# Two-layer encoder with mixture of experts on one Trainium2 core: VectorE forms the low parts of an expert's weights a whole unit at a time

## What is computed

```python
for l in range(DEPTH):
    xn = rms_norm(x, attn_norm[l])
    proj = xn @ w_in[l]
    ...
    x = x + mixed @ w_out[l]
    x = x + moe_ffn(rms_norm(x, ffn_norm[l]), w_router, router_bias, w_gate[l], w_up[l], w_down[l])

def moe_ffn(h, w_router, router_bias, wg, wu, wd):
    ...
    hg = jnp.einsum('nd,edf->nef', t, wg)
    hu = jnp.einsum('nd,edf->nef', t, wu)
    act = jax.nn.silu(hg) * hu * combine[:, :, None].astype(t.dtype)
    out = jnp.einsum('nef,efd->nd', act, wd)
```

## Time and profile before

| | us |
|---|---|
| median of 3 runs | 1950.42 (1948.66 to 1955.75) |
| the profiled execution | 1956.39 |
| its span, first to last instruction | 1954.2 |
| PE busy | 1848.6 |
| DVE busy | 1581.5 |
| ACT busy | 1438.5 |
| mean granted clock of TensorE | 0.974 |

### The profile page before, as it was taken

One profiled execution on the slowest core, in us unless ns is written; L12 is line 12 of the kernel. 1 busy time (PEld: TensorE's weight loads), 2 busy tenths in 40 slices (PEclk: granted clock), 3 DMA queues, 4 the chain that ended last, 5 costly groups with the idle time before them and its releaser, 6 DMA issues.

```text
span 1954.2 us, 30129 instructions
## 1 busy us (share of the span) xinstructions
PE 1848.6 (95%) x8762; PEld 1494.0 (76%) x8762; DVE 1581.5 (81%) x2248; ACT 1438.5 (74%) x2279; POOL 104.6 (5%) x86
## 2 busy tenths in 40 slices
PE   7999999997999999989999999999979999999998
PEld 6887888886677777778778878888867777777775
DVE  5566777657999999999974667775589999999998
ACT  5465666445899999899765646664468999999995
POOL 0000000001010111000000000000010110100000
PEclk9999999996999999999999999999979999999999
DMA  7654444565999999999856444345569999999997
GB/s 271 212 186 141 161 162 155 183 230 201 380 420 420 421 422 421 422 421 419 346 209 243 155 151 161 141 173 194 215 237 409 420 421 421 421 420 418 421 420 270
DMA packets 86699, 582.07 MB, mean 298 GB/s; under 512 B 13612, under 2 KB 13868, under 8 KB 18896
## 3 DMA queue, kind: packets, MB, share of 16 engines
q1 hardware_dynamic: 75600, 542.01, 70.4%
q0 software_dynamic: 11008, 38.95, 5.3%
HBM read 575.91 MB, written 29.36 MB: 310 GB/s over the span
## 4 chain that ended last, share of the span: by engine, by line
PE 58%; DMA 14%; DVE 10%; issue 10%; ACT 7%; ACTq 0%; DVEq 0%; SPq 0%; POOL 0%; POOLq 0%
PE bank L877 12%; PE bank L879 11%; PE bank L878 11%; DMA proj<-in_expert_units 8%; DMA raw<-in_expert_units 5%; PE bank L1032 4%; PE bank L1034 4%; DVE wl L1232 3%; ACT wh L590 3%; PE bank L1051 2%; PE bank L1053 2%; PE bank L1052 2%; DVE xl L1232 2%; PE bank L1023 2%; ACT rows L807 1%
## 5 line engine op out<-in xcount | busy, mean ns | idle before, releaser
L1224 DVE TENSOR_TENSOR wl<-raw,wh 128x1024 fp32r<-128x1024 f32 x256 | 310.1, 1222 | 229.9 <-ACT wh L581 229.6
L581 ACT ACTIVATE wh<-raw 128x1024 fp32r<-128x1024 f32 x256 | 269.0, 1056 | 268.5 <-PE bank L879 266.3
L877 PE MATMUL bank<-wh,xh 128*128 128x512 f32 x1024 | 417.1, 407 | 2.5 <-DVE wl L1224 2.4
L879 PE MATMUL bank<-wh,xl 128*128 128x512 f32 x1024 | 403.3, 394 | 0.0
L878 PE MATMUL bank<-wl,xh 128*128 128x512 f32 x1024 | 401.8, 392 | 0.0
L1232 DVE TENSOR_TENSOR wl<-raw,wh 128x1024 fp32r<-128x1024 f32 x256 | 301.2, 1218 | 22.3 <-ACT wh L590 22.0
L1232 DVE TENSOR_TENSOR wl<-proj,wh 128x1024 fp32r<-128x1024 f32 x256 | 300.6, 1217 | 14.9 <-ACT wh L590 14.6
L590 ACT ACTIVATE wh<-raw 128x1024 fp32r<-128x1024 f32 x256 | 260.0, 1052 | 30.3 <-PE bank L1053 11.6
L590 ACT ACTIVATE wh<-proj 128x1024 fp32r<-128x1024 f32 x256 | 260.5, 1052 | 22.1 <-PE bank L1053 11.0
L1032 PE MATMUL bank<-wh,xh 128*128 128x512 f32 x648 | 267.7, 413 | 4.9 <-DVE xh L1672 3.0
L1034 PE MATMUL bank<-wl,xh 128*128 128x512 f32 x648 | 259.9, 401 | 0.0
(11 more groups left out here) (258 smaller groups left out, 2720.8 us busy)
## 6 DMA issues: line engine op xcount, KB each, us to landing
raw<-in_expert_units SPq DMA_DIRECT2D x192, 1024.0 KB, 13.7
proj<-in_expert_units SPq DMA_DIRECT2D x192, 1024.0 KB, 14.2
raw<-in_in_units SPq DMA_DIRECT2D x96, 1024.0 KB, 4.9
raw<-in_out_units SPq DMA_DIRECT2D x32, 1024.0 KB, 4.8
expert_rows<-rows POOLq DMA_DIRECT2D x4, 1024.0 KB, 4.5
proj<-picks POOLq DMA_DIRECT2D x4, 1024.0 KB, 7.9
x<-in_x SPq DMA_DIRECT2D x2, 1024.0 KB, 7.3
wide<-in_norms POOLq DMA_DIRECT2D x2, 1024.0 KB, 4.9
```

Of the source, the lines that this page charges most:

```text
L581: act_(wh[:, h % CUT, :], ring[j][:, h % 2 * HALF:(h % 2 + 1) * HALF], ACT.Copy)\
L877: mm(out, xh[:, at, tok], rh, start=start, stop=False)
L879: return mm(out, xl[:, at, tok], rh, start=False, stop=stop)
L1224: v.tensor_tensor(wl[:, h % CUT, :], ring[(first + h // 2) % slots][:, h % 2 * HALF:(h % 2 + 1) * HALF], wh[:, h % CUT, :].bitcast(F32), A ...
```

## The change

VectorE's `part_cut` does nothing at an even half. At an odd half it waits for the high parts of both halves and subtracts the whole unit, 128 x 2048, into two neighbouring places, and raises `lo_ready` by two. ScalarE's and TensorE's programs stay as they are.

```diff
@@
+        high_unit = [wh[:, j:j + 2, :].rearrange("p k n -> p (k n)") for j in range(0, CUT, 2)] + \
+            [spare_cut[:, 0:2, :].rearrange("p k n -> p (k n)")]
+        low_unit = [wl[:, j:j + 2, :].rearrange("p k n -> p (k n)") for j in range(0, CUT, 2)] + \
+            [spare_cut[:, 2:4, :].rearrange("p k n -> p (k n)")]
@@
             def part_cut(h, at, kind):
 
-                j = part_slot(h, kind)
-                e.wait_ge(S["hi_ready"], t_.due("hi_ready"))
-                v.tensor_tensor(low[j], ring[(at + h // 2) % DEEP][:, h % 2 * HALF:(h % 2 + 1) * HALF],
-                                high[j].bitcast(F32), ALU.subtract).then_inc(S["lo_ready"], 1)
+                if h % 2 == 0:
+                    return
+                j = part_slot(h - 1, kind) // 2
+                e.wait_ge(S["hi_ready"], t_.due("hi_ready", 2))
+                v.tensor_tensor(low_unit[j], ring[(at + h // 2) % DEEP], high_unit[j].bitcast(F32),
+                                ALU.subtract).then_inc(S["lo_ready"], 2)
```

## The result

| | before | changed |
|---|---|---|
| median, us (4 runs each, compared on one chip) | 1952.49 (1948.66 to 1955.75) | **1989.77** (1983.49 to 1990.31) |
| ratio, 95% interval | | 1.0186 (1.017 to 1.0203) |
| the profiled execution, us | 1956.39 | 1989.8 |
| its span, us | 1954.2 | 1987.5 |

The change costs 37 us by the medians and 33.3 us by the spans of the two profiled executions. The forecast for the difference between the profiled executions was +28.3.

The account below looks back on a forecast made before the run. It took a loop of TensorE, ScalarE and VectorE as the bound. Rounds +12.5 and +14.0, start +2.4 and tail -0.6 sum to +28.3 us: 1984.7 for the profiled execution, median 1979, range 1960 to 2003.

Parts of the forecast that it names:

- The loop of three engines: TensorE, ScalarE and VectorE around down half 8: a round grows from 30.13 to 31.93 us, 14 rounds taking 447.0.
- VectorE's saving costed at nothing: VectorE's wider subtractions save about 0.07 us per unit, 27 us in all, counted as no gain.
- The link: Weight loads in the expert phases: 31.7 us needed per expert against the loop's 31.93, so they hide nothing.
- One of the signs of being right: Bandwidth in the expert phase was to stay within 1% of what it was.
- Rival 3: Expert rounds: the link hides the longer loop, rounds stay at 31.0 us, only the start's +2.4 remains: 1953; chance 0.12.
- The start: First step of each layer: TensorE's first half 8 comes at 506.5 instead of 505.24, +1.2 us per layer.
- The tail: After the last half 8 of a layer: TensorE works without a gap, behind VectorE, so pairs add nothing.
- The last term: Adds in layer 1's tail: their 0.6 us wait for a load goes, -0.6 us.
- The median: Whole kernel: 1984.7 us for a profile like the one before, which lay 6 above its median; so 1979.
- Rival 2: TensorE's waits in expert rounds lower its clock, 1.7 us lost in half of 28 rounds, +24: 2003; chance 0.12.
- The wait before half 8: TensorE idle before the down projection's first matmul, about 1.7 us per expert, put down to VectorE.
- Rival 4: Expert rounds: VectorE's own queue is the bound, 27 us go, gathers under 30 us apart: 1924; chance 0.04.

Follow-up runs that it names:

- run 1: The change, but halves 8 and 9 of every middle and last step cut one at a time again; 1961.5 us, 1.0039 of before.
- run 2: The kernel before, with only halves 8 and 9 of every middle and last step cut as a pair; 2013.5 us, 1.0308 of before.
- run 3: The change, with ScalarE's fourth store moved from after half 8 to after half 9; 1965.1 us, 1.0068 of before.
- run 4: The kernel before, all units by halves, with VectorE's small pieces in the change's order; 1950.9 us, 0.9994 of before.
- run 9: Halves alone with VectorE's pieces in the change's order, plus ScalarE's fourth store after half 9; 1952.8 us, 1.0 of before.
- run 8: The change with pairs only in middle steps and not for 8-9, halves elsewhere, fourth store after half 9; 1950.0 us, 0.9991 of before.
- run 5: The change, with VectorE at halves again in the last step and the end of each layer; 1977.0 us, 1.0132 of before.
- run 7: The change, with one more VectorE instruction per round before the pair of halves 8 and 9; 2015.1 us, 1.0317 of before.
- run 6: The kernel of run 2, with ScalarE's fourth store after half 9 in place of before it; 1957.2 us, 1.0029 of before.

## Why the prediction was right, and where it was off

**The loop of three engines: right, to 0.02 us.** Forecast 31.93 us a round, measured 31.91, and 446.8 us for 14 rounds against 447.0. Its parts came out one by one: 18.80 us to half 3 (forecast 18.79), 10.7 from there to the end of half 9 (10.76), 2.45 from the end of half 9 to TensorE (2.38), and ScalarE's wait of 0.64 us gone. That the sum comes out to 0.02 is partly luck: the second part came 0.09 shorter and the third 0.07 longer. Runs 1, 2 and 3 show that it is this loop: taking the one pair out gives 31.0, leaving it in alone gives 31.9, and taking 0.7 us of ScalarE's work out of it gives 31.07.

**VectorE's saving costed at nothing: right.** It is busy 1560.7 us instead of 1581.5, and its idle time before the pairs grew to 40 us for one group alone (the group above; 22 before). The instruction took 2289 ns. The Trainium skill (VectorE: DVE Perf Modes, The TRN2 errata) gives 2291 ns for a float32 addition of two tensors of this width: the trace agrees. Of the two rules of the Trainium skill (Perfetto Trace Analysis, Optimizing Scalar/DVE Operations), grouping where an engine is saturated and breaking up where one that is not causes bubbles on others, the trace agrees with the second: 384 instructions fewer and 37 us more.

**The link: right that it hides nothing, its pace read too high.** I had it need 31.7 us per expert, from 60 us late in the phase. Over 520 to 850 us of the same trace the queue of the weights moved 132.96 MB, which is 31.2 us for twelve units, and in runs 4 and 9 it moved the same (132.96 and 132.92 MB). The rounds came through faster than that, eleven in 338.9 to 339.9 us, 30.8 to 30.9 each, in all three kernels; the growing landing time fits a stock that is used up meanwhile. Over the 14 rounds of before the mean is 31.0. One of the signs of being right failed with it: the bandwidth was to stay within 1%, and fell from 419 to 411 GB/s, 1.9%. Rival 3 would have held for a loop of up to about 31.0: that is run 8. The price of the whole change is therefore only the part of the loop above this mean, 0.9 us of the 1.5 by which early rounds grew.

**The start: right.** TensorE's first half 8 came at 506.46 (forecast 506.5); counted from the gather ahead of it, it is 1.4 us later in each layer than before, where 1.2 were forecast. Behind the block of table work TensorE waited 2.92 us (0.93 before), which the forecast did not have, and the granted clock was 1.2 GHz for 3.41 us there in each layer; half 8 came as forecast all the same (timeline of PE):

```profile
491.23 0.80 PE L1036 MATMUL bank<-wh,xh 128*128 128x512 f32 x1 [2.92 <-DVE wl L1238]
```

**The tail: wrong.** The step that failed is "After the last half 8 TensorE works without a gap and is behind VectorE, so pairs add nothing". It had two gaps, 1.96 and 1.27 us, at the pairs 14-15 and 20-21, and from the last half 8 to VectorE's last low part it took 31.39 us instead of 28.34: 3.05 per layer, 6.1 in all. The forecast looked at TensorE's work there and not at the hand-overs: VectorE's pair needed the later of two high parts, and TensorE had only 2.9 us of other work. In run 5, with halves there, it takes 28.44. Per phase the books close: forecast 13.7 and 15.2 us, measured 16.7 (496.1 - 479.5) and 18.2 (496.2 - 478.0), the tail's 3.05 apart in each. The last term, 0.6 us less in the adds of layer 1, came: the third add, at 1972.54, has no wait now (timeline of DVE).

**The median.** With the tail the sum is 34.4 against 33.3 between the two profiled executions; the 1.1 between them lies within what the parts outside the phases vary by. I set the median 6 us under it because the profiled execution of before lay 6 above its median; that of after lay on its median, so the medians are 37 apart. The forecast of 1979 was 10.8 us low: 6.1 for the tail and 6 for this step, less the 1.1.

**Rival 2, the lower clock: right that it stayed away, and nearer than its chance said.** The wait before half 8 was forecast at 1.7 us and was 1.25; TensorE also waits 0.29 us for the pair 6-7 just ahead, which the forecast did not have (timeline of PE). Half a microsecond more before half 8, and eight of 28 rounds have such a stretch (run 7).

**Rivals 3 and 4** would have shown landing times of 17 us early, or gathers under 30 us apart; the landing time is 8.1 us even late, and from the second expert on no two gathers stand less than 31.8 us apart.

## What to carry to other kernels

When engines hand a piece of work round in a loop, as here, a wider instruction costs twice, with its own length and with the wait for its last input, but only at the places where the receiver has run out of other work. Follow the loop and cost each such place, tails and starts too, since they have fewer pieces between the hand-overs than the steady rounds. Widen the instructions that have slack around them (run 8 kept eleven pairs in twelve for nothing), and move whatever stands between the two inputs of the wide one out of the way (run 3 took back 25 of 37 us with one number). Ask too what the resource behind the loop is worth: here loops of 29.8, 30.45 and 31.0 us gave the same time, and the 0.84 us by which run 3's loop of 31.07 is shorter than the change's came back in full, 14 times per layer (496.1 to 484.3).

## What the runs showed of the hardware

- A wait of TensorE of under 2 us was enough to lower its granted clock to 1.2 GHz for 3.41 us: after 1.84 us in eighteen rounds of 28 (run 2), after 1.77 in eight (run 7), after 1.25 in none (the change); after 1.94 to 1.96 in the tail in two cases of eight, and after 2.72 at the first half 8 in all four (runs 2 and 6). In run 2 each cost its round 1.55 us (33.46 against 31.91). A kernel whose rounds all wait alike can thus lose some rounds and not others.
- Because of that, fewer wide instructions can cost more than many: with one pair in twelve TensorE ran ahead of it and waited in one piece (2013.5 us), with all twelve the wait was spread over several places (1989.8 us).
- The part of the program between the two expert phases took between 482.7 and 488.4 us in the eleven profiled executions.
